# Five edits to the seams of a fused float32 transformer-and-recurrence kernel on one Trainium2 core

## What is computed

```python
def rms_norm(x, g):
    return x * lax.rsqrt(jnp.mean(x * x, axis=-1, keepdims=True) + EPS) * g

merged = sigmoid(gate_a) * (oa @ w_branch_a) + sigmoid(gate_b) * (ob @ w_branch_b)
y = hs * silu(gate)                    # hs: the recurrence over time, 10 blocks
x = x + y @ w_out_a                    # 1,280 -> 1,024
ckr = rms_norm(x, norm_kv) @ w_dkv     # key-value latents
u = rms_norm(x, norm_b) @ w_in_b       # query latents and gate
x = x + (attention * silu(gate)) @ w_out_b
return rms_norm(x, final_norm)
```

## Time and profile before

| | us |
|---|---|
| median of 3 runs (2796.53 to 2798.96) | 2797.47 |
| the profiled execution | 2798.33 |
| span of its trace | 2796.3 |
| TensorE busy in it | 2657.9 |
| VectorE, GpSimd, ScalarE busy | 1300.7, 879.8, 719.2 |
| mean granted TensorE clock | 0.98 of full |

### The profile page before, as it was taken

How to read it: one execution, slowest core, us unless ns; L and a number is a source line. 1 busy time by engine, 2 the same in 40 slices (tenths; PEclk the granted TensorE clock), 3 DMA queues, 4 the chain that set the end, 5 groups by cost and what they waited for, 6 DMA issues and landing times. The chain is left out here.

```text
span 2796.3 us, 33364 instructions
## 1 busy us (share of the span) xinstructions
PE 2657.9 (95%) x13072; PEld 2194.7 (78%) x13072; DVE 1300.7 (47%) x1648; ACT 719.2 (26%) x941; POOL 879.8 (31%) x660
## 2 busy tenths in 40 slices
PE   6999999899899999999999999999998999898986
PEld 5888887677688888888888878788786778788875
DVE  4475533466453322123212464577845225555543
ACT  5144244222221200000000123455524122212221
POOL 3454423111233333333333443333343222110111
PEclk9999999999999999999999999999999999999998
DMA  3100121101341111111111112211133110000021
GB/s 125 46 31 31 42 72 38 53 35 46 147 143 46 49 49 47 51 45 53 45 53 46 68 53 83 87 45 45 45 127 112 42 56 29 19 10 15 23 83 68
DMA packets 44499, 160.72 MB, mean 57 GB/s; under 512 B 4720, under 2 KB 9072, under 8 KB 41968
## 3 DMA queue, kind: packets, MB, share of 16 engines
q1 hardware_dynamic: 38336, 124.53, 13.1%
q10 hardware_dynamic: 6064, 34.78, 3.3%
HBM read 138.33 MB, written 20.97 MB: 57 GB/s over the span
## 5 line engine op out<-in xcount | busy, mean ns | idle before, releaser
L428 POOL TENSOR_TENSOR derived_vectors<-w_staged 1x1 f32<-1x1 f32 x208 | 51.1, 246 | 1820.5 <-PE ps L544 1308.4
L431 POOL TENSOR_TENSOR w_low<-w_staged,w_high 128x1024 fp32r<-128x1024 f32 x208 | 557.3, 2679 | 16.7
L542 PE MATMUL ps<-h_ffn_high,w_high 128*128 128x512 f32 x832 | 324.6, 390 | 1.6 <-DVE ple_proj L1778 1.6
L544 PE MATMUL ps<-h_ffn_high,w_low 128*128 128x512 f32 x832 | 323.7, 389 | 0.0
L543 PE MATMUL ps<-h_ffn_low,w_high 128*128 128x512 f32 x832 | 323.7, 389 | 0.0
L607 PE MATMUL ps<-h_mix_high,w_high 128*128 128x512 f32 x688 | 281.9, 410 | 0.0
L609 PE MATMUL ps<-h_mix_high,w_low 128*128 128x512 f32 x688 | 269.2, 391 | 0.0
L608 PE MATMUL ps<-h_mix_low,w_high 128*128 128x512 f32 x688 | 268.1, 390 | 0.0
L429 POOL CAST w_high<-w_staged 128x1024 fp32r<-128x1024 f32 x208 | 215.0, 1034 | 0.0
L1760 DVE TENSOR_TENSOR squares<-ps,rstd 128x512 f32<-128x512 f32 x88 | 60.5, 689 | 322.1 <-PE ps L544 311.7
L542 PEld LDWEIGHTS ps<-h_ffn_high,w_high 128*128 128x128 f32 x832 | 156.2, 188 | 34.9 <-issue 2.5
(11 more groups left out here) (344 smaller groups left out, 5388.1 us busy)
## 6 DMA issues: line engine op xcount, KB each, us to landing
w_staged<-weights_in SPq DMA_DIRECT2D x200, 512.0 KB, 3.4
gates_loaded<-gates ACTq DMA_DIRECT2D x8, 1024.0 KB, 7.4
gates<-gates_staged_late SPq DMA_DIRECT2D x24, 256.0 KB, 2.0
x_in<-xT_in SPq DMA_DIRECT2D x4, 1024.0 KB, 9.5
x_mid<-xT_in ACTq DMA_DIRECT2D x1, 4096.0 KB, 12.8
x_spill_rnn<-x_mid ACTq DMA_DIRECT2D x8, 512.0 KB, 2.6
x_late<-x_spill_rnn ACTq DMA_DIRECT2D x4, 1024.0 KB, 7.8
x_spill_mla<-x_late ACTq DMA_DIRECT2D x1, 4096.0 KB, 11.1
```

The costliest lines, as they stand in the source:

```text
L428: nc.gpsimd.tensor_tensor(derived[0:1, 72:73], w_staged[0:1, j, 0:1], w_staged[0:1, j, 0:1], ALU.add)
L431: nc.gpsimd.tensor_tensor(w_low[:, j], w_staged[:, j], f32(w_high[:, j]), ALU.subtract).then_inc(s_split, 1)
L542: nc.tensor.matmul(ps[:, bank], wH, rhs[0][:, r, tok], start=(n == 0), stop=False)
L544: last = nc.tensor.matmul(ps[:, bank], wL, rhs[0][:, r, tok], start=False, stop=last_chunk)
```

## The change

It has five parts.

- First loads. x comes in eight loads of one chunk (`s_xe` for even, `s_x` for odd chunks). ScalarE and VectorE wait for the vectors alone (`s_vec`), and TensorE waits for the two matrices after unit 0.
- Last gates. The two stores of `gates2` unit 9 leave SP's list. ScalarE issues them, ahead of the load of x.
- Last recurrent read. Block 9 is taken out of VectorE's loop, and in it `project(n, 1, rgate)` stands before `recurrence(n - 1)`.
- Key-value inputs. Regions 1 and 4 change places for the tiles of the latent stage, so `h5H` lies in region 4. ScalarE writes `h5H` beside the squares in `wo2`. VectorE writes `h5L` of chunks 0 to 3 there too, into slots 4 to 7, and chunks 4 to 7 after it. `dkv` waits accordingly.
- Final norm. The last chunk's square and sum go by token halves. TensorE sums the first half inside the last `wob` unit. Each half gets its own logarithm and exponential. Output chunks are written and stored by token halves (8 stores of 512 KB).

```diff
-        h5H, h5L = full("h_kv_high", 1, F32R), full("h_kv_low", 2, F32R)
-        h6H, h6L = full("h_mla_high", 0, F32R), full("h_mla_low", 4, F32R)
+        h5H, h5L = full("h_kv_high", 4, F32R), full("h_kv_low", 2, F32R)
+        h6H, h6L = full("h_mla_high", 0, F32R), full("h_mla_low", 1, F32R)
@@ SP
-                sp.dma_start(x1[:, 2 * k:2 * k + 2], a["xT"][:, 2 * k:2 * k + 2]).then_inc(s_x[k], 16)
+                sp.dma_start(x1[:, 2 * k], a["xT"][:, 2 * k]).then_inc(s_xe[k], 16)
+                sp.dma_start(x1[:, 2 * k + 1], a["xT"][:, 2 * k + 1]).then_inc(s_x[k], 16)
...
-                    if 0 <= t < STAGE[stage][2]:
+                    if 0 <= t < min(STAGE[stage][2], 9):
                         store_gates(stage, t)
...
-            for h in range(4):
-                sp.wait_ge(s_fin, 2 * (h + 1))
-                sp.dma_start(a["outT"][:, 2 * h:2 * h + 2], out_sb[:, 2 * h:2 * h + 2]).then_inc(s_out, 16)
+            for h in range(2):
+                for k in range(4):
+                    sp.wait_ge(s_fin, DC * h + 2 * (k + 1))
+                    sp.dma_start(a["outT"][:, 2 * k:2 * k + 2, half_of(h)], out_sb[:, 2 * k:2 * k + 2, half_of(h)]).then_inc(s_out, 16)
@@ TensorE
                         for n, (c, r) in enumerate(chunks):
-                            chunk(h, n, c, r)
+                            chunk(h, n, c, r, low_chunk and low_chunk(r))
+                            if between and h == 1 and n == 4:
+                                between()
...
-            gemm("dkv", (h5H, h5L), low(5), norm(4, 4))
+            def kv_ready(r):
+                return (s_l, 32 + r + 1) if r < 4 else (s_l, 40 + r - 4 + 1)
+            gemm("dkv", (h5H, h5L), kv_ready, norm(4, 4), low_chunk=lambda r: (r + 4) % DC)
...
-            gemm("wob", (y7H, y7L), lambda r: (s_y7l, r + 1))
-            norm(5, 7)()
+            def last_sum(h):
+                pe.wait_ge(s_fsum, h + 1)
+                nc.tensor.matmul(ps[:, 4 + h], ones[:], acc[:, half_of(h)], start=True, stop=True).then_inc(s_nsum, 1)
+            gemm("wob", (y7H, y7L), lambda r: (s_y7l, r + 1), between_last=lambda: last_sum(0))
+            last_sum(1)
@@ ScalarE
+            for h in range(2):
+                act.wait_ge(s_free[bank_of("gates2", 9, h)], use_of("gates2", 0, 9) + 1)
+                act.dma_start(a["gates"][gate_unit("gates2", 9)][:, half_of(h)], gates_late[:, h]).then_inc(s_gst[h], 16)
             act.wait_ge(s_mm, MM_PER_UNIT * STAGE["merge"][0])
             act.dma_start(x2[:], a["xT"]).then_inc(s_x2, 16)
...
-            split_x(4, x4, None, 0, updated("wo2"))
-            split_x(5, x4, h5H, G_KV, None, False)
+            split_x(4, x4, h5H, G_KV, updated("wo2"))
...
-            split_x(7, x5, None, 0, updated("wob"))
-            norm_rstd(5)
+            split_x(6, x5, None, 0, updated("wob"), late=4, n=DC - 1)
+            act.wait_ge(s_l, 52 + 6)
+            for h in range(2):
+                act.wait_ge(s_free[bank_of("wob", 1, h)], use_of("wob", 3, 1) + 1)
+                nc.scalar.activation(sq[:, 1, half_of(h)], x5[:, DC - 1, half_of(h)], ACT.Square).then_inc(s_fsq, 1)
+                nc.scalar.activation(derived[0:1, 73:74], eps[0:1], ACT.Ln)
+                act.wait_ge(s_nsum, 2 * 5 + h + 1)
+                inverse_root([(rstd[:, half_of(h)], ps[:, 4 + h], 1.0 / D, s_rstd)])
@@ VectorE
+                if last:
+                    project(n, 1, rgate)
                 if not first:
                     recurrence(n - 1)
-                project(n, 1, rgate)
+                if not last:
+                    project(n, 1, rgate)
...
-            split_x(4, x4, None, None, 0, add_to("wo2", x4))
-            split_x(5, x4, h5H, h5L, G_KV, squares=False)
+            for m in range(DC):
+                add_to("wo2", x4)(m // 2, m % 2)
+                dve.wait_ge(s_h, 32 + m + 1)
+                if m == 0:
+                    last = nc.vector.tensor_copy(acc[:], sq[:, 0])
+                else:
+                    dve.wait_ge(s_l, 32 + m)
+                    last = nc.vector.tensor_tensor(acc[:], acc[:], sq[:, m % 2], ALU.add)
+                if m < 4:
+                    last = kv_low(m)
+                last.then_inc(s_l, 1)
+            for m in range(4, DC):
+                kv_low(m).then_inc(s_l, 1)
...
+            for h in range(2):
+                xm = x5[:, DC - 1, half_of(h)]
+                read("wob", 3, 1, h, lambda p: nc.vector.tensor_tensor(xm, p, xm, ALU.add))
+                dve.wait_ge(s_fsq, h + 1)
+                nc.vector.tensor_tensor(acc[:, half_of(h)], acc[:, half_of(h)], sq[:, 1, half_of(h)], ALU.add).then_inc(s_fsum, 1)
+            for h in range(2):
+                dve.wait_ge(s_rstd, 2 * 5 + h + 1)
+                for m in range(DC):
+                    nc.vector.scalar_tensor_tensor(out=out_sb[:, m, half_of(h)], in0=x5[:, m, half_of(h)], scalar=V(G_FIN + m),
+                                                   in1=rstd[:, half_of(h)], op0=ALU.mult, op1=ALU.mult).then_inc(s_fin, 1)
```

More of the change, by code:

```diff
@@ L282, in fused_kernel @@
         s_free = [sem(f"bank{b}_read") for b in range(4)]
-        s_const = sem("constants_loaded")
+        s_const, s_vec = sem("constants_loaded"), sem("vectors_loaded")
+        s_xe = [sem(f"x_even_loaded{k}") for k in range(4)]
         s_x = [sem(f"x_loaded{k}") for k in range(4)]
@@ L528, in _, with tile @@
         def _(pe):
-            def tile(stage, i, j, slot, width, column, chunks, rhs, first_wait=None):
+            def tile(stage, i, j, slot, width, column, chunks, rhs, first_wait=None, between=None, low_chunk=None):
                 u0, t0, _, inc = base(stage)
@@ L558, in tile, with gemm, unit @@
                         for n, (c, r) in enumerate(chunks):
[L559 to L561 removed]
+                            chunk(h, n, c, r, low_chunk and low_chunk(r))
+                            if between and h == 1 and n == 4:
+                                between()
+            def gemm(stage, rhs, ready, hook=None, chunk0=0, between_last=None, low_chunk=None):
                 u0, t0, n, T, C = STAGE[stage]
[L565 removed]
+                def unit(i, j, between=None):
                     pe.wait_ge(s_split, 2 * i + (j + u0 + 1))
                     first = isinstance(i, int) and i == 0 and j == 0
[L568 removed]
+                    tile(stage, i, j, (u0 + j) % 2, P, 0, [(c, chunk0 + c) for c in range(C)], rhs, ready if first else None, between, low_chunk)
                     if first and hook:
                         hook()
[L571 to L580 removed]
+                if between_last:
+                    items_of(pe, n - 2, unit)
+                    unit(n // 2 - 1, 0)
+                    unit(n // 2 - 1, 1, between_last)
+                else:
+                    items_of(pe, n, unit)
             def low(q):
@@ L1010, in _, with split_x @@
             pe.wait_ge(mla.outL, 64)
-            gemm("wob", (y7H, y7L), lambda r: (s_y7l, r + 1))
-            norm(5, 7)()
+            def last_sum(h):
[3 more added lines that the diff above has]
+            last_sum(1)
         @block.scalar
         def _(act):
-            def split_x(q, x, H, gain, ready=None, squares=True):
+            def split_x(q, x, H, gain, ready=None, squares=True, late=0, n=DC):
                 def chunk(i, j):
@@ L1387, in low_of, with split_x @@
                 return nc.vector.tensor_tensor(L, source, f32(H), ALU.subtract)
-            def split_x(q, x, H, L, gain, before=None, after_h=True, squares=True):
+            def split_x(q, x, H, L, gain, before=None, squares=True, late=0, n=DC):
                 def chunk(i, j):
@@ L1822, in rnn_block @@
             def rnn_block(n):
-                first = isinstance(n, int)
+                first = isinstance(n, int) and n == 0
+                last = isinstance(n, int) and n == RB - 1
                 w = lambda k: vec[:, bass.ds(4 * n + (V_CW + k), 1)]
@@ L1846, in _ @@
             rnn_block(0)
-            with dve.Fori(1, RB) as n:
+            with dve.Fori(1, RB - 1) as n:
                 rnn_block(n)
+            rnn_block(RB - 1)
             for j in range(2):
```

74 lines of the change are left out of this document (32 added, 42 removed).

## The result

The changed kernel takes 2773.8 us (median of 5 runs, 2763.1 to 2776.5). Beside it the kernel before took 2797.9. The ratio is 0.9909, with an interval of 0.9889 to 0.9929, so it is faster by 25 us (20 to 31), or by 24.1 between the medians. Four of the five runs took 2773.3 to 2776.5 and one took 2763.1. The forecast was 2769, 28.7 less than its profiled execution. The profiled execution of the changed kernel took 2773.8 as well, with a span of 2772.0, against 2796.3 before: 24.3 less.

The account below looks back on a forecast made before the run. TensorE, busy 2657.9 of 2796.3 us, was taken as the bound, so only its idle and slow places pay. Gains 2.8 + 11.7 - 1.3 + 8.0 + 7.5 = 28.7 off 2798.33 gave 2769.6, median 2768.8, stated as 2769; range 2761 to 2777.

Parts of the forecast that it names:

- has the same length and moves by 2.8: Start: VectorE's chain from 11.52 to TensorE's first norm sum keeps its length and comes 2.8 us earlier.
- 3.9 as its bound: Last recurrent read: a loss of 3.9 us if the second wait, about 2.4, lowers the clock as long ones do.
- the wait is handed on: End of the recurrence: TensorE, released early, stands again until about 2032.8 and before 2051; the pair ends 1.27 us later.
- a possible gain of 0.5: Last recurrent read: the other bound, a gain of 0.5 us if GpSimd's stretch of VectorE there shrinks.
- small pieces: First loads and output stores: small pieces are served one after the other without overlap, giving 2783 us; chance 0.04.
- the held store: Merge: x's load still holds the last gate store, so the merge gains nothing, giving 2780.7 us; chance 0.08.
- the moved read that pays: End of the recurrence: the moved read gains 6.9 us in full instead of -1.3, giving 2760.8 us; chance 0.06.
- The slower case: End: output stores with 2 KB rows take 6 us each, giving 2804 us; chance 0.02.

## Why the prediction was right, and where it was off

The direction, the range and the size hold: 24.1 measured against 28.7, and the time 4.8 above the forecast. One thing was luck: the latent attention took 338.7 and 338.4 in the two traces that were compared, where later kernels took 333.7 to 334.4, and the working had nothing for it.

- First loads, forecast 2.8: 2.75 at the `probs_band` wait in the trace of the changed kernel, but 2.2 between the medians of all traces with and without the new loads, so the close match is partly luck. The working was right at its start (7.5 against 7.54; the half piece landed 1.2 earlier). The first sum came 2.6 earlier. Alone the part showed only 0.7 at the end. The step that the chain "has the same length and moves by 2.8" left out that a few microseconds of clock can swallow it.
- Last gates, forecast 11.7: 11.95. The store was no longer held. It landed 2.2 after its issue (forecast 2.0 to 2.5), and the low part took 0.6 more than my 1.22, which didn't matter. The profile after has no wait here.
- Last recurrent read, forecast a loss of 1.3, with 3.9 as its bound: 6.8 in the trace, 8.3 by the medians. This is the mis-sized term, and it is outside its own bound. The mechanism was named: the wait is handed on, TensorE stands twice, the chain of the last block is the bound. I wrote that TensorE stands a second time "before 2051", and put this wait at about 2.4 for the bound. It was 5.95. Of the 4.2 us by which the adds came later, counted from the first `wo1` matmul, 1.1 is the delay (`y_high` of block 8 came 1.24 later, as forecast). The other 3.1 is the last recurrence's stretch beside GpSimd. I had this stretch in the working only as a possible gain of 0.5. The rows that would have warned me were there: in the kernel before, the scan of block 8 took 3.14 and that of block 9 took 2.29, the same operation. With the longest rows of that trace for all three (3.14, 3.09, 3.42 against 2.29, 2.01, 2.22) I would have had the 3.1. The last 2.6 came behind the adds: from TensorE's restart there to the last matmul of `wo2` it is 84.1 us instead of 81.5, because it restarts at the lower clock.
- Key-value inputs, forecast 8.0 (7.0 to 8.9): 8.2 in the trace, 9.0 alone. The wait of 7.4 stayed.
- Final norm, forecast 7.5 (5.5 to 8.6): 7.8, both in the changed kernel and alone. The two rules of the Trainium skill: by "ScalarE: Activation LUTs", section "What ACT_TABLE_LOAD costs", a switch takes about 2.66 us. The table load between the two roots took 1.28 again, and the output ran on without a gap (10.68 for 16), so the load as it is was hidden. With the longer switch, by an estimate, the second root would be ready at 2763.5 (2761.53 + 0.63, and 1.38 more), about 0.6 after VectorE came to the ninth output (2757.62 + 8 x 0.66), so it would not have been hidden. By "DMA: Bandwidth & Descriptors", section "Bandwidth", the smaller stores should have suffered. Each did move less per microsecond (512 KB in 3.0 against 1 MB in 4.1), but they overlapped, and the end came earlier.

The rivals: small pieces fell with those stores; the held store fell with the landing of 2.2; the moved read that pays fell for the changed kernel, as taking it out won 8.3 us. It does pay, 4.7 us by the medians and 6.6 by the traces, once the adds don't stand behind the recurrence. The slower case fell.

## What to carry to other kernels

When a read is moved ahead, follow the next work of its engine to the next release that TensorE needs, and move that too: here the move alone lost 4 to 8 us, and it gained about 5 once the adds and the reloads had been moved as well. Price an operation at the longest duration that its kind has in the trace, and not at the one it had in this place, when another engine's periodic work will shift against it. And put a part of a few microseconds to the test in more than one trace before counting it, since the clock after an unrelated wait can give it or take it.

## What was not expected of the hardware

- VectorE and GpSimd stretch each other, and by much. Beside a low part of GpSimd 18 of 19 scans and 25 of 25 products were long, and without one none of 121 and 115. The scan took 2.29, 3.14 or 4.38 us, the product of 128x1024 1.22, 2.0 or 3.25, the low part 1.22, 2.2 or 3.4. GpSimd's low part of a unit took 2.3 to 4.5. In the changed kernel this moved the end of the recurrence by 3.1 us.
- A store of 256 KB took 12.2 us when issued 0.8 us after a 4 MB load on another queue, and 2.2 when issued 0.4 us before one on the same queue.
- The same kernel falls into two groups of times about 5 us or more apart (2754.5 to 2755.3 and 2759.7 to 2760.0; 2796.0 and 2801.9 to 2804.9 for the moved read alone; 2763.1 and 2773.3 to 2776.5 for the changed kernel).
- After waits of the same length (3.1 to 3.2 us, or 2.53) TensorE starts again at the full clock or at the lower one: rows of 0.39 or 0.58, and 1.35 or 2.51 for twelve matmuls.
